# Column order of the streamed block and of the accumulator in a float32r decoder trunk: runs of four words, 64 bytes apart

## What is computed

```python
def swiglu_ffn(h, w_in, w_out):
    gate, up = jnp.split(h @ w_in, 2, axis=-1)
    return (jax.nn.silu(gate) * up) @ w_out
...
for i in range(DEPTH):
    h = layer_norm(ALPHA * h + 0.5 * swiglu_ffn(h, ffn_w_in[i, 0], ffn_w_out[i, 0]), ...)
    mix = short_conv_mixer(h, ...) if i % 2 == 0 else gla_mixer(h, ...)
    h = layer_norm(ALPHA * h + mix, ...)
    h = layer_norm(ALPHA * h + 0.5 * swiglu_ffn(h, ffn_w_in[i, 1], ffn_w_out[i, 1]), ...)
return h[:, N_META:]
```

## Time and profile before

| | us |
|---|---|
| median of 3 runs | 1018.05 |
| lowest, highest | 1017.97, 1018.32 |
| the profiled execution, its own time | 1018.94 |
| its span, first to last instruction | 1017.1 |
| granted TensorE clock, mean | 0.998 |

### The profile page before, as it was taken

One profiled execution on the slowest core, in us unless ns is written; L12 is line 12 of the kernel. 1 busy time (PEld: TensorE's weight loads), 2 busy tenths in 40 slices (PEclk: granted clock), 3 DMA queues, 4 the chain that ended last, 5 costly groups with the idle time before them and its releaser, 6 DMA issues.

```text
span 1017.1 us, 19130 instructions
## 1 busy us (share of the span) xinstructions
PE 1006.5 (99%) x7932; PEld 988.9 (97%) x7932; DVE 721.3 (71%) x1077; ACT 510.7 (50%) x743; POOL 122.2 (12%) x136
## 2 busy tenths in 40 slices
PE   9999999999999999999999999999999999999997
PEld 7999999999999999999999999999999999999986
DVE  5855657689889865557697565667897999766443
ACT  5644344465456543445565344445867766544340
POOL 2000002320002000003220000133152420000000
PEclk9999999999999999999999999999999999999999
DMA  9965656637752866556638665555255738866531
GB/s 254 260 191 173 180 155 178 188 91 208 228 173 81 254 184 176 169 161 178 195 90 255 176 185 154 170 163 162 84 145 143 206 109 249 246 189 200 174 125 42
DMA packets 324264, 176.60 MB, mean 174 GB/s; under 512 B 6658, under 2 KB 320048, under 8 KB 324176
## 3 DMA queue, kind: packets, MB, share of 16 engines
q1 hardware_dynamic: 323664, 174.15, 58.5%
q0 software_dynamic: 480, 1.15, 0.4%
q10 hardware_dynamic: 32, 0.07, 0.0%
HBM read 174.29 MB, written 1.05 MB: 172 GB/s over the span
## 4 chain that ended last, share of the span: by engine, by line
PE 92%; DVE 4%; ACT 1%; POOL 1%; DMA 1%; issue 1%; SPq 0%; DVEq 0%; POOLq 0%; ACTq 0%
PE bank L1310 24%; PE bank L1315 24%; PE bank L1313 23%; PE bank L1329 3%; PE bank L1331 3%; PE bank L1330 3%; PE bank L1469 2%; PE bank L1471 2%; PE bank L1470 2%; PE bank L1354 2%; PE bank L1355 2%; PE bank L1356 2%; DVE weights_lo L823 1%; DMA raw_weights<-in_ffn_w_in_dram 1%; DVE rms L1223 1%
## 5 line engine op out<-in xcount | busy, mean ns | idle before, releaser
L464 ACT ACTIVATE weights_hi<-raw_weights 128x1024 fp32r<-128x1024 f32 x335 | 354.0, 1060 | 413.7 <-PE bank L1315 299.1
L823 DVE TENSOR_TENSOR weights_lo<-raw_weights,weights_hi 128x1024 fp32r<-128x1024 f32 x334 | 414.8, 1248 | 203.1 <-ACT weights_hi L464 201.9
L1310 PE MATMUL bank<-x_hi,weights_hi 128*128 128x272 f32 (+1 forms) x1584 | 227.4, 286 | 0.0
L1315 PE MATMUL bank<-x_lo,weights_hi 128*128 128x272 f32 (+1 forms) x1584 | 225.9, 285 | 0.0
L1313 PE MATMUL bank<-x_hi,weights_lo 128*128 128x272 f32 (+1 forms) x1584 | 224.6, 284 | 0.0
L1310 PEld LDWEIGHTS bank<-x_hi,weights_hi 128*128 128x128 f32 x1584 | 207.1, 188 | 0.6 <-ACT consts L628 0.2
L1315 PEld LDWEIGHTS bank<-x_lo,weights_hi 128*128 128x128 f32 x1584 | 206.8, 188 | 0.0
L1313 PEld LDWEIGHTS bank<-x_hi,weights_lo 128*128 128x128 f32 x1584 | 206.0, 188 | 0.0
L1310 PE MATMUL bank<-mid_hi,weights_hi 128*128 128x272 f32 x462 | 68.2, 288 | 0.0
L1313 PE MATMUL bank<-mid_hi,weights_lo 128*128 128x272 f32 x462 | 68.1, 288 | 0.0
L1315 PE MATMUL bank<-mid_lo,weights_hi 128*128 128x272 f32 x462 | 68.0, 288 | 0.0
(11 more groups left out here) (230 smaller groups left out, 1213.9 us busy)
## 6 DMA issues: line engine op xcount, KB each, us to landing
raw_weights<-in_ffn_w_in_dram SPq DMA_DIRECT2D x176, 512.0 KB, 4.5
raw_weights<-in_ffn_w_out_dram SPq DMA_DIRECT2D x70, 512.0 KB, 3.5
raw_weights<-in_conv_w_in_dram SPq DMA_DIRECT2D x24, 512.0 KB, 3.9
raw_weights<-in_gla_w_in_dram SPq DMA_DIRECT2D x24, 512.0 KB, 3.8
raw_weights<-in_ffn_w_out_dram SPq DMA_DIRECT2D x24, 384.0 KB, 3.0
raw_weights<-in_conv_w_out_dram SPq DMA_DIRECT2D x8, 512.0 KB, 4.5
raw_weights<-in_gla_w_out_dram SPq DMA_DIRECT2D x8, 512.0 KB, 4.8
x_tok<-in_x_dram SPq DMA_DIRECT2D x2, 512.0 KB, 5.0
```

What stands on the lines that cost most here:

```text
L464: nc.scalar.activation(w_hi[:, n % RING, :], raw[:, n % RAW, :], ACT.Copy).then_inc(hi_split, 1)
L823: nc.vector.tensor_tensor(w_lo[:, s, :], raw[:, n % RAW, :], w_hi[:, s, :].bitcast(F32), ALU.subtract).then_inc(lo_split, 1)
L1310: nc.tensor.matmul(ps, block_of(w_hi, n, k - k0), hi[:, k, cols], start=first and k == k0, stop=False)
L1315: mm = nc.tensor.matmul(ps, block_of(w_hi, n, k - k0), lo[:, k, cols], start=False, stop=last and k == k1 - 1)
```

## The change

Wherever `ps` is 272 wide, and in the last projection at all widths, both the streamed operand and the accumulator are seen through `by_rows`. It takes the row as groups of 16 words (64 bytes), each of four runs of four words, and walks first run 0 of all groups, then run 1 of all, and so on: four passes, in each of them steps of 64 bytes between runs. For 272 words the operand is 4 x 17 x 4, for 512 it is 4 x 32 x 4, for 256 it is 4 x 16 x 4. The stationary operand stays as it was. Since both sides walk alike, each column's sum goes to the same word as before. Products of other widths in `multiply`, `multiply_raw`, the first unit and the products with `minus128` (which add into the same accumulators) are not touched.

```diff
--- before.py
+++ after.py
@@ -1301,18 +1301,23 @@
             def block_of(w, n, k):
                 return w[:, n % RING, k * P:(k + 1) * P]
 
+            def by_rows(ap):
+                return ap.rearrange("p (i j e) -> p j i e", e=4, j=4)
+
             def multiply(ps, n, source, cols, k0=0, k1=KU, first=True, last=True, ready=None, before_last=None, middles=()):
 
                 hi, lo = source
+                walk = by_rows if ps.shape[-1] == T else lambda ap: ap
+                into = walk(ps)
                 if ready is None and before_last is None and not middles:
                     pe.wait_ge(hi_split, n + 1)
                     for k in range(k0, k1):
-                        nc.tensor.matmul(ps, block_of(w_hi, n, k - k0), hi[:, k, cols], start=first and k == k0, stop=False)
+                        nc.tensor.matmul(into, block_of(w_hi, n, k - k0), walk(hi[:, k, cols]), start=first and k == k0, stop=False)
                     pe.wait_ge(lo_split, n + 1)
                     for k in range(k0, k1):
-                        nc.tensor.matmul(ps, block_of(w_lo, n, k - k0), hi[:, k, cols], start=False, stop=False)
+                        nc.tensor.matmul(into, block_of(w_lo, n, k - k0), walk(hi[:, k, cols]), start=False, stop=False)
                     for k in range(k0, k1):
-                        mm = nc.tensor.matmul(ps, block_of(w_hi, n, k - k0), lo[:, k, cols], start=False,
+                        mm = nc.tensor.matmul(into, block_of(w_hi, n, k - k0), walk(lo[:, k, cols]), start=False,
                                               stop=last and k == k1 - 1)
                     mm.then_inc(unit_used, 1)
                     return
@@ -1326,9 +1331,9 @@
                         if k == at:
                             extra()
                     w_h, w_l = block_of(w_hi, n, k - k0), block_of(w_lo, n, k - k0)
-                    nc.tensor.matmul(ps, w_h, hi[:, k, cols], start=first and k == k0, stop=False)
-                    nc.tensor.matmul(ps, w_h, lo[:, k, cols], start=False, stop=False)
-                    mm = nc.tensor.matmul(ps, w_l, hi[:, k, cols], start=False, stop=last and k == k1 - 1)
+                    nc.tensor.matmul(into, w_h, walk(hi[:, k, cols]), start=first and k == k0, stop=False)
+                    nc.tensor.matmul(into, w_h, walk(lo[:, k, cols]), start=False, stop=False)
+                    mm = nc.tensor.matmul(into, w_l, walk(hi[:, k, cols]), start=False, stop=last and k == k1 - 1)
                 mm.then_inc(unit_used, 1)
 
             def mean_total(q, n_tok):
@@ -1465,10 +1470,10 @@
                 def accumulate(k, i, last):
                     b, c0, c1, at = LAST_PARTS[i]
                     toks, cols = slice(META + b * P, META + (b + 1) * P), slice(c0, c1)
-                    ps, slot = bank[at][:, 0:c1 - c0], (OUT_UNIT + k) % RING
-                    nc.tensor.matmul(ps, mid_hi[:, k, toks], w_hi[:, slot, cols], start=False, stop=False)
-                    nc.tensor.matmul(ps, mid_hi[:, k, toks], w_lo[:, slot, cols], start=False, stop=False)
-                    return nc.tensor.matmul(ps, mid_lo[:, k, toks], w_hi[:, slot, cols], start=False, stop=last)
+                    ps, slot = by_rows(bank[at][:, 0:c1 - c0]), (OUT_UNIT + k) % RING
+                    nc.tensor.matmul(ps, mid_hi[:, k, toks], by_rows(w_hi[:, slot, cols]), start=False, stop=False)
+                    nc.tensor.matmul(ps, mid_hi[:, k, toks], by_rows(w_lo[:, slot, cols]), start=False, stop=False)
+                    return nc.tensor.matmul(ps, mid_lo[:, k, toks], by_rows(w_hi[:, slot, cols]), start=False, stop=last)
 
                 pe.wait_ge(resid_ready, KD * LAST_NORM)
                 pe.wait_ge(mid_ready, 4 * KF - 1)
```

## The result

The changed kernel takes 1007.33 us (median of 6 runs, 1006.80 to 1011.05), the kernel before 1018.09 (median of 6, 1017.91 to 1020.98). The ratio is 0.9896, 95% interval 0.9881 to 0.9911: 10.8 us faster. The forecast was 990 us; the range, 962 to 1030, held the time. The profiled execution took 1007.63 us itself, its span is 1005.8 against 1017.1 us, its mean granted clock 0.998 as before.

What follows compares the result with a forecast made beforehand. TensorE bounds the kernel, by products times pitch. Savings of 26.8 us (272-wide), 1.4 and 0.9 us (last projection), less 0.5 us for VectorE, sum to 28.6 us: forecast 990 us, range 962 to 1030.

Steps and rivals of the forecast that it cites:

- Bound and counts: TensorE, busy 99% of the span, sets the time as products times pitch; 5424, 198 and 132 products are touched.
- what I take: 272-wide products of `multiply` reach the packed 256-wide products' excess of 6.4 ns: 119.7 ns each, 26.8 us less.
- The reason behind it: Streamed reads and the next product's weight reads collide in one 64-byte piece; the walk leaves it after 4 columns, not 16.
- the sign of my mechanism: 24 products of `x`, and likewise of `mid`, take 2.87 us instead of 2.98, as start addresses stop mattering.
- telling comparison: 256-wide products: 113.1 ns on the packed copy, 120.0 in the last projection, so about half the excess belongs to addresses.
- The last projection: 512-wide products go from 233.3 to 226.1 ns, 1.4 us less; 256-wide from 120.0 to 113.1, 0.9 us less.
- The cover: VectorE and the load queue keep up with faster TensorE, except VectorE's splits in the GLA stage: 0.5 us back.
- (a): More of the excess goes, halfway to the bare columns: 272-wide products at 116.5 ns, kernel 972 us; chance 0.24.
- (b): No change: the excess comes from the hand-over or the weight load's own reads; 1018 us; chance 0.12.
- (c): Each 64-byte piece entered costs 0.4 ns: 272-wide products at 140.5 ns, kernel 1112 us; chance 0.17.
- (d): Accumulator writes in runs of four fall to 0.86 ns a column: 272-wide 234 ns, some 600 us more; chance 0.06.

## Why the prediction was right or wrong

**Bound and counts: right.** TensorE held the time, the gain is pitch times count, and the 5424 + 198 + 132 products account for 12.4 us of an 11.3 us shorter span. The packed products stayed at 113.1 ns.

**The failed step: "what I take", the 272-wide products at 119.7 ns.** They came to 122.9. The excess fell from 10.9, 12.1 and 13.6 ns to 9.6, not to 6.4, so this term gave 9.5 us where I had put it at 26.8. I took the excess of the best-placed products in the trace for what any placement would reach under the walk. It is not, and it is not even what that placement gives to 272 columns: `x` put at that place, contiguous, stood at 123.3 ns. The walk moves reads by another pattern, with a price of its own. Against the same nest with its reads held, 115.8 ns, that price is 7.1 ns, and the same walk put on the packed block made that worse (113.1 to 114.6).

**The reason behind it: wrong in its main part.** I had the streamed block and the next product's weights meeting in one place. Fewer weight reads take 1.6 or 1.7 ns off the pitch at 272 columns and add 3.6 in the packed products; holding the streamed reads on one word takes 8.4 away. What the walk changes is how the streamed reads follow each other. What was right is that the places of the streamed reads make most of the excess, that columns and hand-over don't (2.5 ns is left), and that `x`, `mid` and `yc` would come together: all three stand at 122.9 in the stretches read. I had named that as the sign of my mechanism; it came although the mechanism fell, and partly by luck, since inside `x` the products of `x_hi` stayed at 123.8 ns and those of `x_lo` went to 121.3. My "telling comparison", 113.1 against 120.0 ns, was also weaker than I took it for: all the 256-wide products of the last projection have a mean of 118.3.

**The last projection: right sign, 512 too small.** 223.3 ns where I said 226.1, so 2.0 us for 1.4; the 256-wide ones at 113.3 for 113.1, 0.9 us as said, in the stretch read, and 0.6 us over all of them.

**The cover.** DVE holding the GLA stage, 0.5 us: its two stretches stayed as they were. I did not name GpSimd, which turned 1.5 us of the gain into a wait for `sT`. The account leaves 1.1 us that did not arrive, and TensorE's listed waits grew by 1.5.

**The rivals.** (a) did not happen under the walk, but the 115.8 ns exist, with reads that don't move. (b), no change, is off by 10.8 us. (c) priced a new piece at 0.4 ns; the walk's 68 runs with the address held cost nothing, and the pitch fell. But a loss was within reach: the same edit with steps of 128 or 256 bytes makes 512-wide products 11 and 43 ns slower than contiguous ones. (d) fell: the accumulator alone in runs of four left the kernel at 1018.09. Its price was also misread: the two rows of 0.22 us are the two records of one 256-wide float32 product, which thus takes 0.44 us, 1.7 ns a column. The Trainium skill's first sentence, in "Advanced Engine Details and Errata", section "Memory Cachelines", that any non-contiguous PSUM pattern slows products, does not hold here for runs of four float32 words 64 bytes apart; its second, that two consecutive elements should be contiguous, is compatible with it, though nothing here tried single elements.

**Still open.** Why 64 bytes is the best step, how much of the loss at long steps is the accumulator's or the number of passes', and what makes one set of addresses run at 126.7 ns in one FFN and at 120.0 in another. The addresses and the line alone don't decide it. Loads that run beside it, or the phase in which one product's reads meet those of the next, could; neither was tried.

## What to carry to other kernels

Where TensorE bounds a kernel with float32r products, compare the pitch of equal widths at different places in the timeline. A difference at one width hints at the streamed reads, though not always at their addresses (126.7 and 120.0 ns above), and streaming one word for all columns tells in a single run how much of it there is to win (here 46 us). Changing the order of the streamed reads wins only part of it, and wins or loses by the step: measure the step, do not reason it from the best placement, and leave blocks alone that already lie well. Placement and walk are two settings of the same thing, so try them together.

## What was not expected of the hardware

- The order of the columns, in the stream and the accumulator together, is worth 53 ns of 512 columns: 223.3 ns at steps of 64 bytes, 276.7 at 256, 265.6 at 512, 233.3 contiguous.
- Reading one piece of 64 bytes over and over is slower than reading a whole row: 129.2 against 124.2 ns for 272 columns; with the address held on each run of four for 17 runs it is 115.8.
- Loading a quarter of the stationary columns saves 1.7 ns of 124.2 on `x` and costs 3.6 on 113.1 in the packed blocks.
- The same tensors at the same line, with the weights in the same slots, run at an even 126.7 ns in the first FFN and an even 120.0 in the third.
